# Expert groups of 32 tokens in four strips of the array, in place of 64 in two

## The reference

```python
def _moe(t, w_router, b_router, w_gu, b_gu, w_down, b_down):
    logits = (tok @ w_router + b_router).astype(jnp.float32)
    top_val, top_idx = lax.top_k(logits, TOP_K)          # 4 of 32 experts for each token
    top_w = jax.nn.softmax(top_val, axis=-1)
    ...
    def expert_block(args):
        rows, wts, e = args
        hgu = tok[rows] @ w_gu[e] + b_gu[e]              # (.., 1024) @ (1024, 2048)
        gate = jnp.minimum(hgu[:, 0::2], SWIGLU_LIMIT)
        up = jnp.clip(hgu[:, 1::2], -SWIGLU_LIMIT, SWIGLU_LIMIT)
        act = (up + 1.0) * (gate * jax.nn.sigmoid(SWIGLU_ALPHA * gate))
        y = act @ w_down[e] + b_down[e]                  # (.., 1024) @ (1024, 1024)
        return y.astype(jnp.float32) * wts[:, None]
```

## Time and profile before

| what | us |
|---|---|
| median of 3 runs | 1435.06 (1433.96 to 1435.71) |
| span of the profiled execution, first to last instruction | 1426.0 |
| PE busy with matmuls | 1328.5 (93%) |
| DVE, ACT busy | 281.0, 252.5 |
| weights moved in the whole execution | 455.91 MB, mean 320 GB/s |
| L918 (up), 2176 instructions | 482.9 |
| L947 (down), 1088 instructions | 245.9 |

### The profile page before, as it was taken

The page is one execution under the profiler, slowest core; times in us unless marked ns, Lnnn a source line. Parts: engine busy times, 40 slices in busy tenths (PEclk is TensorE's granted clock), DMA queues, the critical chain, the costliest instruction groups (busy, mean ns, idle before and its releaser), DMA issues.

```text
span 1426.0 us, 15909 instructions
## 1 busy us (share of the span) xinstructions
PE 1328.5 (93%) x6068; PEld 624.0 (44%) x6069; DVE 281.0 (20%) x832; ACT 252.5 (18%) x515; POOL 24.6 (2%) x36
## 2 busy tenths in 40 slices
PE   5999999999979999999999999999999999998898
PEld 3574777877543333333333333333333233332322
DVE  2243424543141111111012011110111101111011
ACT  1115422253010111111101111111011110111111
POOL 2100000000000000000000000000000000000000
PEclk9999999999989999999999999999999999999998
DMA  8832246321399899995967999999999999999992
GB/s 313 314 122 89 85 152 236 119 78 60 118 353 375 330 418 418 416 418 229 417 245 301 418 416 416 418 418 418 417 416 418 418 419 418 416 416 418 418 415 89
DMA packets 96277, 455.91 MB, mean 320 GB/s; under 512 B 4964, under 2 KB 10232, under 8 KB 63448
## 3 DMA queue, kind: packets, MB, share of 16 engines
q1 hardware_dynamic: 95204, 453.50, 79.4%
q0 software_dynamic: 656, 1.46, 0.3%
q10 hardware_dynamic: 388, 0.55, 0.1%
HBM read 454.45 MB, written 1.05 MB: 319 GB/s over the span
## 4 chain that ended last, share of the span: by engine, by line
PE 43%; DMA 26%; ACT 1%; issue 1%; DVE 0%; SPq 0%; DVEq 0%; ACTq 0%
DMA ring<-in_w_down 26%; PE bank L918 20%; PE bank L947 14%; PE bank L889 3%; PE bank L881 3%; PE bank L905 3%; ACT mq L1209 1%; PE bank L936 1%; ACT sp_ L1199 0%; PE bank L974 0%; PE bank L836 0%; DVE sc L1590 0%; PE bank L824 0%; PE bank L862 0%; SPq L350 0%
## 5 line engine op out<-in xcount | busy, mean ns | idle before, releaser
L918 PE MATMUL bank<-ring,sp_ 128*64 128x512 f32 x2176 | 482.9, 602 | 0.0
L918 PEld LDWEIGHTS bank<-ring,sp_ 128*64 128x64 f32 x2176 | 155.2, 139 | 325.3 <-issue 325.3
L947 PE MATMUL bank<-ring,mq 128*64 128x512 f32 x1088 | 245.9, 600 | 43.2 <-DMA ring<-in_w_down 24.1
L947 PEld LDWEIGHTS bank<-ring,mq 128*64 128x64 f32 x1088 | 76.1, 137 | 191.3 <-issue 151.7
L1631 DVE TENSOR_SCALAR sp_<-bank 128x256 f32<-128x256 f32 x68 | 28.6, 420 | 574.6 <-PE bank L918 574.6
L531 PE MATMUL bank<-ring 128*128 128x512 f32 x288 | 124.8, 593 | 3.4 <-DMA ring<-in_w_mem_kv 1.8
L1205 ACT ACTIVATE sp_<-sp_ 128x256 f32<-128x256 f32 x68 | 28.3, 417 | 512.8 <-DVE sp_ L1631 512.8
L652 PE MATMUL bank<-ring 128*128 128x256 f32 x448 | 99.6, 381 | 0.0
L652 PEld LDWEIGHTS bank<-ring 128*128 128x128 f32 x448 | 84.2, 190 | 11.9 <-issue 0.7
L531 PEld LDWEIGHTS bank<-ring 128*128 128x128 f32 x288 | 54.4, 190 | 70.1 <-issue 68.0
L1647 DVE TENSOR_SCALAR sp_<-cst,rank_it,w_it 128x64 f32<-128x64 f32 x68 | 16.7, 310 | 287.4 <-PE bank L918 287.4
(11 more groups left out here) (289 smaller groups left out, 763.4 us busy)
## 6 DMA issues: line engine op xcount, KB each, us to landing
ring<-in_w_gu SPq DMA_DIRECT2D x128, 2048.0 KB, 23.1
ring<-in_w_down SPq DMA_DIRECT2D x64, 2048.0 KB, 20.0
ring<-in_w_in SPq DMA_DIRECT2D x13, 2048.0 KB, 11.0
ring<-in_w_mem_kv SPq DMA_DIRECT2D x2, 2048.0 KB, 10.3
ring<-in_w_out SPq DMA_DIRECT2D x2, 2048.0 KB, 9.1
ring<-in_cmp_w_k SPq DMA_DIRECT2D x1, 2048.0 KB, 8.5
ring<-in_cmp_w_v SPq DMA_DIRECT2D x1, 2048.0 KB, 9.1
ring<-in_w_br_mem SPq DMA_DIRECT2D x1, 2048.0 KB, 7.3
```

The costliest lines, as they stand in the source:

```text
L918: mm = nc.tensor.matmul(BH[b][64 * hh:64 * hh + 64, :], xgT[:, k, 64 * par:64 * par + 64], w[:, c, o:o + 512], start=False, stop=k == KT - ...
L947: mm = nc.tensor.matmul(BG[64 * hh:64 * hh + 64, :], actT[:, o:o + 64], w[:, c, 512 * hh:512 * hh + 512], start=k == 0, stop=k == KT - 1, ...
```

## The change

`SLOT_TOK` becomes 32, and the loop runs over single groups (`item`). In `up` the weights are 128x32, and the 2048 output columns lie in four strips of 32 columns of the array, all in one bank `BH`. The number of matmuls for a group is the same as before (32 in the source for up, 16 for down). The bias comes after `part(0)` and no longer before it. `down` uses four strips as well: even and odd k in different strips, so that `BY` holds two partial sums for each half of the output. `y_sb` is one copy of 128x512, and `Gw` holds the weights four times side by side, so that `scatter` adds the partial sums up: it uses rows 0 to 63 for the left half and rows 64 to 127 for the right one, in 4 matmuls of the source. Gather (16 in the source, streaming 32 columns each and no longer 128), scatter, the four transposes and all copies are now done once for each group. The PE order of a group is up, scatter (of the group before), gather (of the next), down. The counting of groups in the router's tail uses one comparison with a table `limits`. The load order on SP and the ring are the same.

```diff
-SLOT_TOK = 64
+SLOT_TOK = 32
@@ PE
             def gather():
-                for half, b in ((1, BX), (0, BG)):
-                    for c in range(4):
-                        for i in range(NT):
-                            o = P * (4 * half + c)
-                            mm = nc.tensor.matmul(b[:, P * c:P * c + P], x2[:, i, o:o + P], Gm[:, i, :],
-                                                  start=i == 0, stop=i == NT - 1)
-                    mm.then_inc(S("g_full"), 1)
-            def scatter(last=False):
+                for c in range(KT):
+                    for i in range(NT):
+                        mm = nc.tensor.matmul(BG[:, SLOT_TOK * c:SLOT_TOK * c + SLOT_TOK], x2[:, i, P * c:P * c + P], Gm[:, i, :],
+                                              start=i == 0, stop=i == NT - 1)
+                mm.then_inc(S("g_full"), 1)
+            def scatter(final=False):
                 for t in range(NT):
                     for hh in range(2):
-                        mm = nc.tensor.matmul(ACC[t][hh][:, :], STs[:, P * t:P * t + P],
-                                              y_sb[:, 512 * hh:512 * hh + 512], start=False, stop=last, skip_group_check=True)
+                        r = slice(64 * hh, 64 * hh + 64)
+                        mm = nc.tensor.matmul(ACC[t][hh][:, :], STs[r, P * t:P * t + P], y_sb[r, :],
+                                              start=False, stop=final, skip_group_check=True)
@@ in up
-                        for b in range(2):
-                            for hh in range(2):
-                                o = 1024 * b + 512 * hh
-                                mm = nc.tensor.matmul(BH[b][64 * hh:64 * hh + 64, :], xgT[:, k, 64 * par:64 * par + 64],
-                                                      w[:, c, o:o + 512], start=False, stop=k == KT - 1,
-                                                      skip_group_check=True)
+                        for j in range(4):
+                            mm = nc.tensor.matmul(BH[32 * j:32 * j + 32, :], xgT[:, k, :], w[:, c, 512 * j:512 * j + 512],
+                                                  start=k == 0, stop=k == KT - 1, skip_group_check=True)
+                def parts(row, first):
+                    pe.wait_ge(brow_in[row], e * 8 + (8 if row else 16))
+                    part(0, first)
+                    bias(row)
+                    for q in range(1, TWICE):
+                        part(q, first + q)
@@ down
-                pe.wait_ge(S("act_ready"), i * 2 + 2)
-                for q in range(4):
-                    mm = nc.tensor.transpose(BX[:, P * q:P * q + P], act_sb[:, P * q:P * q + P], ident)
+                pe.wait_ge(S("act_ready"), i + 1)
+                for h in range(2):
+                    nc.tensor.transpose(BT[:, P * h:P * h + P], ut[:, P * h:P * h + P], ident)
+                pe.wait_ge(S("Gw_ready"), i + 1)
+                for t in range(NT):
+                    mm = nc.tensor.transpose(BT[:, 256 + P * t:256 + P * t + P], Gw[:, t, :], ident)
...
-                        o = P * (2 * (k // 4) + k % 2) + 64 * ((k // 2) % 2)
+                        o = P * (k % 2) + 32 * (k // 2)
                         for hh in range(2):
-                            mm = nc.tensor.matmul(BG[64 * hh:64 * hh + 64, :], actT[:, o:o + 64],
-                                                  w[:, c, 512 * hh:512 * hh + 512],
-                                                  start=k == 0, stop=k == KT - 1, skip_group_check=True)
+                            g = 2 * hh + k % 2
+                            mm = nc.tensor.matmul(BY[32 * g:32 * g + 32, :], actT[:, o:o + 32], w[:, c, 512 * hh:512 * hh + 512],
+                                                  start=k < 2, stop=k >= KT - 2, skip_group_check=True)
@@ the loop body in place of pair
+            def item(i, final=False):
+                e = pe.value_load(idx[0:1, bass.ds(i + NE, 1)], min_val=0, max_val=NE - 1)
+                odd = pe.value_load(idx[0:1, bass.ds(i + (NE + ITEMS), 1)], min_val=0, max_val=1)
+                pe.wait_ge(S("g_evac"), i + 1)
+                up(e, odd)
+                pe.wait_ge(S("st_evac"), i + 1)
+                pe.wait_ge(S("y_evac"), i + 1)
                 scatter()
                 if not final:
-                    pe.wait_ge(S("G_ready"), j + 2)
+                    pe.wait_ge(S("G_ready"), i + 2)
                     gather()
...
+                down(i, e)
@@ ACT, one group
+            def item(i, final=False):
+                act.wait_ge(S("g_clip"), i + 1)
+                nc.scalar.activation(sg, gt, ACT.Sigmoid, scale=ALPHA).then_inc(S("g_sig"), 1)
+                if not final:
+                    tokens(i + 1)
                 act.wait_ge(S("a_full"), i + 1)
-                nc.scalar.activation(actT, BX[:, :], ACT.Copy).then_inc(S("a_evac"), 1)
+                nc.scalar.activation(actT, BT[:, 0:256], ACT.Copy).then_inc(S("a_evac"), 1)
+                nc.scalar.activation(STs, BT[:, 256:512], ACT.Copy).then_inc(S("st_evac"), 1)
                 act.wait_ge(S("down_done"), i * 2 + 2)
+                nc.scalar.activation(y_sb, BY[:, :], ACT.Copy).then_inc(S("y_evac"), 1)
@@ DVE, one group
+            def item(i):
+                dve.wait_ge(S("gu_done"), i * 4 + 1)
                 for t in range(NT):
+                    ins = V.tensor_scalar(Gw[:, t, :].rearrange("p (g n) -> p g n", g=4), mid(C("iota")[:, 0:SLOT_TOK], 4), rank_it[:, t, bass.ds(i, 1)], w_it[:, t, bass.ds(i, 1)],
+                                          ALU.is_equal, ALU.mult)
                 ins.then_inc(S("Gw_ready"), 1)
+                onehot(i + 1)
+                activate(i)
```

More of the change, by code:

```diff
@@ L300, in hybrid_layer @@
         r_f, r_B, r_g, r_M, r_nm = (rows[:, 256 * n:256 * n + 256] for n in range(5))
[L303 to L312, removed]
+        Gm = sp_[:, 0:64].rearrange("p (i n) -> p i n", i=NT)
+        Gw = sp_[:, 64:320].rearrange("p (i n) -> p i n", i=NT)
+        STs = sp_[:, 320:576]
+        xgT = sp_[:, 576:832].rearrange("p (c n) -> p c n", c=KT)
+        gt, ut, sg = (sp_[:, a:a + 256] for a in (832, 1088, 1344))
+        y_sb = mq[:, 0:512]
+        actT = mq[:, 512:768]
         brow = (bg0[32:33, :], bg0[64:65, :])
@@ L326, in hybrid_layer @@
         Eit = bg1[0:32, 1312:1312 + ITEMS]
[L327 to L331, removed]
+        Ait = bg1[0:32, 1376:1376 + ITEMS]
+        more = bg1[0:32, 1440:1440 + SEQ // SLOT_TOK]
+        nlast = bg1[0:1, 1456:1457]
+        before = bg1[0:1, 1472:1472 + NE]
         ACC = [[banks[2 * i + h] for h in range(2)] for i in range(NT)]
-        BG, BX, BH = banks[4], banks[5], [banks[6], banks[7]]
+        BH, BG, BT, BY = banks[4:8]
         out_t = out[0].rearrange("(i p) d -> p i d", p=P)
@@ L971, in pair @@
                     pe.wait_ge(S("bdn_in"), 16)
-                    for i in range(NT):
+                    for t in range(NT):
                         for hh in range(2):
-                            nc.tensor.matmul(ACC[i][hh][:, :], rTs[:, 256 + P * i:256 + P * i + P],
+                            nc.tensor.matmul(ACC[t][hh][:, :], rTs[:, 256 + P * t:256 + P * t + P],
                                              b_dn[:, 512 * hh:512 * hh + 512], start=False, stop=False, skip_group_check=True)
[L976 to L983, removed]
+                down(i, e)
             pe.wait_ge(S("G_ready"), 1)
@@ L988, in _ @@
             pe.wait_ge(S("idx_ready"), 1)
-            last_pair = pe.value_load(idx[0:1, NE + 2 * ITEMS:], min_val=NE // 2 - 1, max_val=ITEMS // 2 - 1)
-            with pe.Fori(0, last_pair) as j:
-                pair(j)
-            pair(last_pair, final=True)
+            last_item = pe.value_load(idx[0:1, NE + 2 * ITEMS:], min_val=NE - 1, max_val=ITEMS - 1)
+            with pe.Fori(0, last_item) as i:
+                item(i)
+            item(last_item, final=True)
             pe.wait_ge(S("last_y"), 1)
-            scatter(last=True)
+            scatter(final=True)
         @block.scalar
@@ L1192, in _ @@
             ins.then_inc(S("lg_exp"), 1)
-            def tokens(n):
-                for k, (half, b) in enumerate(((1, BX), (0, BG))):
-                    act.wait_ge(S("g_full"), n + (k + 1))
-                    nc.scalar.activation(xgT[:, 4 * half:4 * half + 4, :].rearrange("p c n -> p (c n)"), b[:, :],
-                                         ACT.Copy).then_inc(S("g_evac"), 1)
-            def gates(i):
-                for b in range(2):
-                    act.wait_ge(S("g_clip"), i * 2 + (b + 1))
-                    nc.scalar.activation(sg[b], gt[b], ACT.Sigmoid, scale=ALPHA).then_inc(S("g_sig"), 1)
@@ L1232, in _ @@
-            with act.Fori(0, last_pair) as j:
-                pair(j)
-            pair(last_pair, final=True)
-            nc.scalar.activation(sg[0][:, 0:1], sg[0][:, 1:2], ACT.Copy).then_inc(S("last_y"), 1)
+            last_item = act.value_load(idx[0:1, NE + 2 * ITEMS:], min_val=NE - 1, max_val=ITEMS - 1)
```

(17 more changed lines are left out.)

101 lines of the change are left out of this document (26 added, 75 removed).

## The result

The changed kernel takes 1491.98 us (median of 4 runs, 1489.12 to 1497.19) against 1435.3; the ratio is 1.041, with a 95% interval of 1.038 to 1.044. It is slower, within the forecast range, and 21 us above the forecast of 1471.

A forecast was written before the change was run, and what follows sets the result against it. The prediction took the kernel as bound by weight streaming, with holes where PE is in experts with several groups. Span 1426.0 + 54.4 (stream) - 18.2 (end) = 1462.2, plus 9.1 around the span: 1471 us, 8-in-10 range 1442 to 1512.

The forecast's parts named there:

- The mechanism: Weight stream: stops while PE is still in an expert with several groups; single-group experts go at the stream's pace, 30.5 us.
- The period's terms: PE's time for one new group with its chunks there: seven parts, from up to the loop turn, summing to 18.6 us.
- the loop's turn: Between groups: branch and register loads not hidden behind down, 0 to 1.6 us, taken as 0.5 us a group.
- The lower bound of 17.3: Low end of the 17.3 to 21.5 us given for one new group's PE time; used for the range's 1442.
- The single place of the earlier trace: Trace at 254.84 us: L739 on rows 64 to 127 runs beside L746 on rows 0 to 63; basis for scatter's 1.9.
- The clock within a group: Experts 6 to 9: no time was added for a falling TensorE clock inside their groups.
- rival 2: Clock falls within every group, also in experts 6 to 9, after gather: 1.7 us a fall, + 26 us, 1497; chance 0.13.
- The long stretch: Experts 6 to 9, 11 groups, ten PE periods: stream loses 76.4 us, against 40.8 us before the change.
- The five single experts: Experts 12, 15, 19, 22, 24, two groups each: stream loses 0.5 us each, plus 2.5 us each for the low clock.
- the prediction's sign: Sign listed for a wrong forecast: PE idle before up that no transfer explains would be the turn of the loop.
- The start: Expert 1 and the start: stream loss as today, 7.7 us, taken as 9 us.
- The end: Behind the last chunk: 8.8 us of work plus 3.5 for half speed, 12.3 us in place of 30.5, 18.2 us won.

The follow-up runs named there:

- the cut kernels: Changed kernel and kernel before, each cut to one group for each expert, further tokens left out: 1372.39 us (ratio 0.958) and 1397.3 us (0.975).
- The wider gather: Changed kernel with gather streaming 64 columns (each one-hot matrix twice) in place of 32: 1473.08 us, ratio 1.028.
- the turned gather: Changed kernel with the one-hot matrix as gather's weight and tokens streaming: 1438.9 us, ratio 1.004; placed ahead of scatter as well, 1434.87 us, 1.002.

## Why the forecast came out as it did

By spans, the forecast was 1462.2 and 1487.3 was measured: 25 us short. The steps one by one; the losses of the stream are against 417 GB/s, as in the windows above.

- **The mechanism** (PE's period in experts with several groups sets the holes, single ones ride on the stream) was right; the cut kernels show it, and so do the kernels with other gathers, whose time falls with the period (19.4, 18.3, 15.6 us).
- **The period's terms.** Up 7.0 (1.72 + 5.29; forecast 6.9), bias 0.99 (1.1), scatter 1.92 (1.9), gather 3.69 (3.5), gather's end to down 1.02 (676.80 - 675.78; 1.1), down 3.64 (3.6), the loop's turn nothing in the stretch (0.5). Together 18.26 for 18.6. The lower bound of 17.3 follows from no term: with scatter at 1.8 and no turn of the loop it is 18.0. With 17.3 the range's lower end comes to 1445 by the prediction's own terms, not 1442. The single place of the earlier trace rows was enough to price the row halves; with full overlap up runs at 7.0/64 = 0.110 us for an instruction, a quarter of the 0.434 of full width. (The Trainium skill, "TensorE: Matmul & The Clock Gate", section "Packing small matmuls", has 3.07 times for four tiles in rows and 2.38 for three in columns; the four column strips here ran at 3.96.)
- **The clock within a group** is the step that was mis-sized: forecast nothing, measured 19.4 - 18.26 = 1.15 us on average over ten periods. That was rival 2, in two of three groups, so its truth lies between the forecast and the rival. The reason given against rival 2, a clock of 1.00 in the earlier trace rows, came from gathers that stream 128 columns and says nothing of 32. The long stretch lost 87.2 us for 78.9: ten periods are 11.5 us longer by the clock and 3.4 shorter by the other terms, so two misses partly cancelled. The wider gather removes the falls there: 16.7 + 60.4 us lost from 640 to 820.
- **The five single experts** lost 22.3 us in all, where 15 was forecast: besides the clock there is 0.64 us of idle before up when the half down before it had to wait for its chunk, which no transfer explains; by the prediction's sign that is the loop's turn. Timeline of the changed kernel in expert 12:
```profile
889.48 1.92 PE L942 MATMUL bank<-ring,mq 128*32 128x512 f32 x16 [1.47 <-DMA ring<-in_w_down]
892.05 1.92 PE L907 MATMUL bank<-ring,sp_ 128*32 128x512 f32 x16 [0.64 <-issue]
...
902.10 4.32 PE L876 MATMUL bank<-sp_,sc 128*128 128x32 f32 x32
...
907.88 5.63 PE L942 MATMUL bank<-ring,mq 128*32 128x512 f32 x32 [0.55 <-ACT mq L1188]
```
  Half of down there took some 3.5 us, done by 911.4, 21.9 us behind the last chunk's landing where 18.1 would have kept the stream running.
- **The start** lost 17.7 us, 9 was forecast: expert 1 has two groups and comes when the stream has no lead. It was put at "as today" and not worked through; that is a term of its own of 9 us.
- **The end** was 13.1 us (12.3), but by other terms, so the agreement is partly luck. Behind the last landing the forecast had 0.3 + 1.9 for half a down, 0.9, 5.7, and 3.5 for half speed. But dn1 landed 8.1 us behind gu3 and not 10.2, so the whole of down came behind it: 0.5 + 5.4, then 0.8 and 6.4. The low clock took 1.7 us of it; the row named for the 3.5 (8.95 in place of 7.09) shows 1.9. The chain:
```profile
1474.74 5.38 PE bank L942 x32
1480.88 1.15 PE bank L885 x4
```
- **Span against median.** I added the 9.1 us between the span before and the median before. For the changed kernel the execution lies only 1.8 us above its span (1489.12 and 1487.3). A later run of the kernel before has a span of 1426.0 as well, and took 1427.85 us. The profiled execution of the kernel before was thus a quick one, by some 7 us, and those 7 us stood in the forecast as start and end. Against medians the kernel is 57 us slower, against profiles 61.

The three misses on the stream (8.3 + 7.3 + 8.7 = 24.3) and 0.8 at the end are the 25 us. In the median it is 21, since the span measured is only 4.7 us under its median and not 9.1.

## What to carry to other kernels

In a kernel that streams its weights, list the work for each piece of weights and not the sum of work: the total of PE's busy time fell here by 56 us and the time rose by 57, since splitting groups moved work from experts that wait for the stream to those the stream waits for. Price a step that is shared between groups before unsharing it: gather was the difference between 4.1% and 0.2%, 1.3 points of it by the falls of the clock and the rest by its length of 3.7 us a group, which stayed the same for 32 and for 64 columns streaming. Here the narrow operand did better as the weight than as the stream (0.86 us for 3.69). And before shortening a piece of work, look at what it covers: half a down hid 1.4 us of idle that a quarter did not.

## What was not expected of the hardware

- A gather of 32 instructions with 128x128 weights and 32 columns streaming, 3.69 us long, brings TensorE's clock to 0.50 for about 3 us in two groups of three; the same with 64 columns streaming (3.72 us long) leaves it at 1.00, and so does the turned gather of 0.86 us (from 640 to 680 us). The single gather-like stretch in the trunk (L620, 24 columns, 3.65 us) shows no fall: the granted clock was 1.00 from 146 to 162 us. What sets the two apart is not settled.
- Fewer matmuls can mean more time at the low clock: without scatter ten downs in a row were slow, where the changed kernel has seven of ten.
- The average clock of 0.80 in the kernel with one group for each expert cost nothing that shows in the stream, which kept 417 GB/s from 440 to 1340 us.
